# Attention values of all sixteen heads computed ahead of the heads, token-major, and the output units in another order

## The chip, the core and the metric

One NeuronCore of a Trainium2 chip runs the whole kernel as one launch. The metric is the device time of that launch in microseconds (us). Engines are called by their short names in the profile: PE (TensorE, matrix products), DVE (VectorE), ACT (ScalarE), POOL (GpSimd) and SP (SyncE, which here only issues DMAs).

## What is computed

One block over 512 tokens of width 2048, float32. First an RMS norm and a mixer of 16 heads of width 128, then an RMS norm and a sparse expert layer (PEER). The change touches the mixer alone:

```python
proj = rmsnorm(x) @ w_in              # q, k, v, gate of 8 heads; q, k, v of 8 heads; 8 forget logits
# heads 0..7 ("fox"): softmax(q k^T * s + c_q - c_k, causal) @ v, times sigmoid(gate);
#                     q and k are RMS-normed per head
# heads 8..15 ("stick breaking"): a = exp(log_sigmoid(z) + suffix sum of log_sigmoid(-z)) @ v
mixed = concat([fox * sigmoid(gate), sb])
h = x + mixed @ w_out
y = h + peer(rmsnorm(h))
```

## The kernel before

Every large product is made of **units**. A unit is one weight tile of 128 x 2048 float32 (1 MB). SP loads it to `raw[k % 2]` (`load`), ACT rounds it to `wh[k % 2]` (`split_hi`, line 399), and POOL, in the later stages DVE, writes the remainder to `wl[k % 2]` (`split_lo`, line 405). PE then makes 48 matmuls of 512 columns: high by high, high by low and low by high. There are two buffers of each kind, so unit k is loaded after the remainder of unit k-2 is made and rounded after unit k-2 is multiplied. The activations stand in SBUF in the same two parts, `xh` and `xl`.

Two forms of unit exist. `gemm` (lines 419 to 421) has the weights stationary and gives 128 output features by 512 tokens in one PSUM bank. `chunk_unit` (lines 444 to 446) has the activations stationary and gives 128 tokens by 512 output features in each of four banks; four such units (q = 0 to 3) add up to one chunk c of 512 features. The output projection uses `chunk_unit`, 16 units, chunks 0 to 3 one after another.

The mixer runs as follows. After the norm comes a small unit for the forget logits. A fox head has four `gemm` units (q, k, v, gate), a stick-breaking head three (q, k, v), 56 in all. PE's instructions are in an order written out by hand: between the units of head h it does the attention steps of head h-1. For a fox head: `logits_pe`, unit, `vturn_pe`, unit, `pturn_pe`, unit, `out_pe`, `sumsq_pe`, unit. For a stick-breaking head: `z_pe`, unit, `vturn_pe`, `tri_pe`, unit, `out_pe`, unit. `vturn_pe` (line 1800) turns the head's values from feature-major to token-major with four transposes; ACT has copied them out of the bank before (`value_act`, line 886) and DVE copies them again after (`vtok_dve`, line 1174).

Each of ACT and DVE has one queue, worked in order. For a stick-breaking head ACT does the absolute value, exponential and logarithm of the scores (lines 925 to 930) and three rounded copies (933), DVE the softplus (1254, 1259) and three remainders (1262), and PE's `tri_pe` waits for all of them.

After the last `gemm` the output of the heads, `mixed`, which occupies the memory of `acc`, is split again into `xh` and `xl` in four quarters: ACT's `mix_split(k)` (line 971) and DVE's `mix_rest(k)` (line 1294), each over 128 x 2048. Quarter q is read by output units q of every chunk. `xh` can only be overwritten when the last `gemm` is done.

The output units need free banks: ahead of the first matmul into a bank, PE waits on the counter `chunk_out` (the argument `prev` of `chunk_unit`). For chunks 0 and 1 the banks are free from the start, and the counter gets its 8 by one DVE instruction:

```python
nc.vector.memset(stat[:, 12:13], 0.0).then_inc(chunk_out, 8)     # line 1302
```

It stands in DVE's queue behind `mix_rest(0)` and `mixed_dve(NSB - 1)` (the copy of the last head's output), and ahead of `mix_rest(1)`, `(2)` and `(3)`. Once quarter tb of `mixed` is split, SP reloads `x` into `acc[:, tb]`; after the four of them it loads the norm's gain, then the further weights.

Of the kernel before, what the change touches and what calls it, by code (L numbers as in the profile page):

```python
# [87 lines left out]
N_FOX = 1  # L88
N_SB = N_FOX + 4 * NFOX
N_OUT = N_SB + 3 * NSB  # L90
# [10 lines left out]
M_PQ = N_OUT  # L101
# [38 lines left out]
def build(nc, x, attn_g, w_f, w_in, b_forget, q_g, k_g, w_out, ffn_g, ffn_row, w_pq, sub_keys, u, v, u_rows,  # L140
          v_rows, out):
    ctx = ExitStack()
    with ctx:
# [48 lines left out]
        q_raw, k_raw, q_sq, k_sq, qn, kn, vT, gT, vtok = (at(512 * i, 512) for i in range(9))  # L192
# [67 lines left out]
        CHUNK_BANKS = [[banks[6], banks[7], banks[4], banks[5]], banks[0:4]]  # L260
        GATE_BANKS = [banks[6], banks[7], banks[3], banks[1]]
# [48 lines left out]
        vt_done = sem("vt_done")  # L310
        vtok_done = sem("vtok_done")
# [229 lines left out]

        def zero(n):
            return isinstance(n, int) and n <= 0
# [35 lines left out]
        def _(sp):  # L579
# [14 lines left out]

            load(sp, N_OUT, w_out[0])
            load(sp, N_OUT + 1, w_out[1])
            load(sp, N_OUT + 2, w_out[2])
            load(sp, N_OUT + 3, w_out[3])
            for tb in range(TB):
# [3 lines left out]
            with sp.Fori(0, 6) as i:  # L603
                for k in (4, 5):
                    load(sp, N_OUT + k, w_out[i * 2 + k], i, 2)
# [218 lines left out]
        def _(act):  # L824
# [38 lines left out]
            def gate_act(p):  # L863

                act.wait_ge(unit_done, p * 4 + 5)
                wait_from(act, mixed_done, p)
                nc.scalar.activation(gT, gemm_bank[0][:], ACT.Exp, scale=-1.0).then_inc(freed[0], 1)
# [9 lines left out]
            def square_act(h, c):  # L877

                act.wait_ge(freed[(1 + c) % 2], h * 2 + (1 + c) // 2 + 1)
# [3 lines left out]
            def value_act(k, i=0, stride=0):  # L883

                act.wait_ge(unit_done, k + 1 + stride * i)
                nc.scalar.activation(vT, gemm_bank[k % 2][:], ACT.Copy).then_inc(freed[k % 2], 1)
# [7 lines left out]
            def fox_act(h, p):  # L894

                if p is not None:
                    gate_act(p)
                split_hi(act, 2, h, 4)
                if p is not None:
                    exp_act(p)  # L900
                else:
                    forget_act()
# [8 lines left out]
            fox_act(0, None)  # L911
            fox_act(1, 0)
            with act.Fori(2, NFOX) as h:
                fox_act(h, h - 1)
# [27 lines left out]
            def stick_pair_act(i, peeled):  # L942
                for r in range(2):
                    k = N_SB + 3 * r
                    s = i * 2 + r
                    if peeled and r == 0:
                        gate_act(NFOX - 1)
                        split_hi(act, k + 1)
                        exp_act(NFOX - 1)
                        query_act(k)  # L950
                        split_hi(act, k + 2)
                        split_hi(act, k + 3)
                    else:
                        value_act(k - 1, i, 6)
                        split_hi(act, k + 1, i, 6)
                        softplus_act(s - 1)
                        query_act(k, i)
                        split_hi(act, k + 2, i, 6)
                        weight_act(s - 1)
                        split_hi(act, k + 3, i, 6)  # L960

            stick_pair_act(0, True)
            with act.Fori(1, NSB // 2) as i:
                stick_pair_act(i, False)
            softplus_act(NSB - 1)
            value_act(N_OUT - 1)
# [8 lines left out]
            weight_act(NSB - 1)  # L975
            for k in (1, 2, 3):
                mix_split(k)
# [10 lines left out]
            for n in range(N_PQ - N_OUT):  # L988
                split_hi(act, N_OUT + n + 1)
                if n in (5, 9, 13):  # L990
                    for tb in range(TB):
                        chunk_square(n // 4 - 1, tb)
# [130 lines left out]
        def _(dve):  # L1123
# [48 lines left out]
            def vtok_dve(a):  # L1172
                dve.wait_ge(vt_done, a + 1)
                nc.vector.tensor_copy(vtok, banks[7][:]).then_inc(vtok_done, 1)

# [5 lines left out]
            def gate_dve(p):  # L1181

                dve.wait_ge(freed[0], p * 2 + 3)
# [24 lines left out]

            def fox_dve(h, p):
                if p is not None:  # L1210
                    max_dve(p)
                    prob_dve(p)
                else:
                    dve.wait_ge(unit_done, 1)
                    nc.vector.tensor_copy(ftmp, gemm_bank[0][32:32 + PH, :]).then_inc(forget_step, 1)
                    dve.wait_ge(forget_step, 3)
                    nc.vector.tensor_tensor(ftmp, gemm_bank[0][0:PH, :], ftmp, ALU.add).then_inc(forget_step, 1)
                    dve.wait_ge(forget_step, 4)
                    nc.vector.tensor_scalar(flog, ftmp, bf[:, 0:1], None, ALU.add).then_inc(freed[0], 1)
                copy_out(1, q_raw, h, 4)  # L1220
                if p is not None:
                    decay_dve(h)
                    vtok_dve(p)
                copy_out(2, k_raw, h, 4)
                if p is not None:
                    turned_dve(p)
                    gate_dve(p)
                else:

                    dve.wait_ge(decay_ready, 6)  # L1230
                    dve.wait_ge(act_step, 3)
                    nc.vector.scalar_tensor_tensor(out=flog, in0=flog, scalar=0.0, in1=ftmp, op0=ALU.min,
                                                   op1=ALU.subtract).then_inc(dve_step, 1)
                    dve.wait_ge(dve_step, 1)
                    nc.vector.tensor_tensor_scan(csum, cr[0:PH].bitcast(F32), flog, 0.0, ALU.mult,
                                                 ALU.add).then_inc(csum_done, 1)
                    dve.wait_ge(csum_done, 1)
                    nc.vector.tensor_copy(csum_hi, csum).then_inc(csum_done, 1)
                    dve.wait_ge(csum_done, 2)
                    nc.vector.tensor_tensor(csum, csum, csum_hi.bitcast(F32), ALU.subtract).then_inc(csum_done, 1)  # L1240
                    dve.wait_ge(csum_done, 3)
                    decay_dve(h)
                rms_dve(h)

            fox_dve(0, None)
            fox_dve(1, 0)
            with dve.Fori(2, NFOX) as h:
                fox_dve(h, h - 1)
# [16 lines left out]
            def mixed_dve(s):  # L1265
                dve.wait_ge(o_done, s + (NFOX + 1))
                nc.vector.tensor_copy(mixed_at(s + NFOX), banks[6][:]).then_inc(mixed_done, 1)

            def stick_pair_dve(i, peeled):
                for r in range(2):  # L1270
                    k = N_SB + 3 * r
                    s = i * 2 + r
                    if peeled and r == 0:
                        max_dve(NFOX - 1)
                        prob_dve(NFOX - 1)
                        vtok_dve(NFOX - 1)
                        turned_dve(NFOX - 1)
                        copy_out(k + 1, kn)
                        gate_dve(NFOX - 1)
                    else:  # L1280
                        softplus_dve(s - 1)
                        vtok_dve(s + (NFOX - 1))
                        copy_out(k + 1, kn, i, 6)
                        mixed_dve(s - 1)

            stick_pair_dve(0, True)
            with dve.Fori(1, NSB // 2) as i:
                stick_pair_dve(i, False)
            softplus_dve(NSB - 1)
            vtok_dve(HEADS - 1)  # L1290
# [18 lines left out]
            for c in range(CH - 1):  # L1309
                add_chunk(dve, N_OUT + 4 * c + 3, 3 * c, c, CHUNK_BANKS[c % 2])  # L1310
# [460 lines left out]
        def _(pe):  # L1771
# [3 lines left out]
            def sumsq_pe(h):  # L1775

                for c, buf in enumerate((q_sq, k_sq)):
# [17 lines left out]
            def vturn_pe(a, k, i=0, stride=0):  # L1795

                evacuated(pe, k, i, stride)
                wait_from(pe, vtok_done, a)
                for j in range(TB):
# [287 lines left out]
```

## Time and profile before

| | |
|---|---|
| time, median of 3 runs | 3244.74 us (3244.32 to 3246.33) |
| the profiled execution's own time | 3248.89 us |
| its span, first to last instruction | 3247.1 us |
| PE busy | 3217.4 us, 99% |
| mean granted TensorE clock | 0.998 |
| mixer units, first matmul to last | 32.96 to 954.21 us of the span |

A matmul's busy time overlaps the next one's: the records show 0.39 us each, while their starts are 0.23 us apart. What PE's work costs is therefore read from the distance between starts in the timeline, not from the busy time. "Idle before" names whose signal ended a wait.

### The profile page before, as it was taken

What the parts mean: (1) busy time and instruction counts of PE and PEld (TensorE: products, weight loads), DVE (VectorE), ACT (ScalarE), POOL (GpSimd) and SP (SyncE); (2) the same over time, 40 slices, a digit from 0 to 9 for tenths busy, and PEclk for the clock granted to TensorE, in tenths of its full rate; (3) what the DMA queues carried; (4) which work ended last, traced back from release to release, by engine and by line L of the source; (5) the groups of instructions that cost most, each with busy time, mean ns of one, the idle gap of its engine ahead of it and who ended that gap; (6) DMA issues with size and microseconds to landing.
All of it is one profiled execution on the core that took longest, in us unless ns stands there. A gap on an engine that the chain in (4) does not pass through costs nothing. (4 is left out here: it accounts for less than half of the span.)

```text
span 3247.1 us, 41510 instructions
## 1 busy us (share of the span) xinstructions
PE 3217.4 (99%) x16730; PEld 2817.9 (87%) x16730; DVE 2263.5 (70%) x2636; ACT 1123.7 (35%) x1172; POOL 933.5 (29%) x424
## 2 busy tenths in 40 slices
PE   8999999999999999999999999999999999999999
PEld 6878778887878899999999899889989988888887
DVE  5666541113027888988874898888888888888887
ACT  5232323334232234566553223222222322222221
POOL 4333333333433331111101223233323321223222
PEclk9999999999999999999999999999999999999999
DMA  3222222223233247899977999889988988888888
GB/s 144 78 78 90 78 78 79 78 78 136 97 117 118 91 145 270 292 329 321 324 237 266 343 342 348 338 336 351 353 330 326 364 346 308 318 337 340 343 320 317
DMA packets 171364, 777.87 MB, mean 240 GB/s; under 512 B 14064, under 2 KB 80752, under 8 KB 86384
## 3 DMA queue, kind: packets, MB, share of 16 engines
q1 hardware_dynamic: 127488, 457.77, 38.6%
q0 software_dynamic: 43776, 318.79, 26.2%
q8 instruction: 60, 0.98, 0.1%
q14 instruction: 40, 0.33, 0.0%
HBM read 731.10 MB, written 44.34 MB: 239 GB/s over the span
## 5 line engine op out<-in xcount | busy, mean ns | idle before, releaser
L419 PE MATMUL bank<-xh,wh 128*128 128x336 f32 (+1 forms) x3184 | 1105.5, 347 | 1.8 <-DVE wl L1128 1.8
L421 PE MATMUL bank<-xh,wl 128*128 128x336 f32 (+1 forms) x3184 | 1090.1, 342 | 0.0
L420 PE MATMUL bank<-xl,wh 128*128 128x336 f32 (+1 forms) x3184 | 1088.1, 342 | 0.0
L399 ACT ACTIVATE wh<-raw 128x2048 fp32r<-128x2048 f32 x344 | 658.1, 1913 | 1001.9 <-PE bank L446 734.9
L1128 DVE TENSOR_TENSOR wl<-raw,wh 128x2048 fp32r<-128x2048 f32 x252 | 576.8, 2289 | 211.2 <-ACT wh L399 210.0
L419 PEld LDWEIGHTS bank<-xh,wh 128*128 128x128 f32 x3184 | 598.9, 188 | 46.9 <-issue 4.0
L405 POOL TENSOR_TENSOR wl<-raw,wh 128x2048 fp32r<-128x2048 f32 x92 | 425.0, 4620 | 741.3 <-ACT wh L399 741.3
L420 PEld LDWEIGHTS bank<-xl,wh 128*128 128x128 f32 x3184 | 599.2, 188 | 44.8 <-issue 1.9
L421 PEld LDWEIGHTS bank<-xh,wl 128*128 128x128 f32 x3184 | 598.2, 188 | 45.1
L444 PE MATMUL bank<-wh,xh 128*128 128x512 f32 x1072 | 417.1, 389 | 0.8 <-DVE stat L1302 0.8
L446 PE MATMUL bank<-wh,xl 128*128 128x512 f32 x1072 | 417.0, 389 | 0.0
L445 PE MATMUL bank<-wl,xh 128*128 128x512 f32 x1072 | 417.0, 389 | 0.0
L811 POOL DMA_INDIRECT arena<-in_u_rows,g_idx x128 | 251.3, 1963 | 453.5 <-DVE acc L1617 221.8
L811 POOL DMA_INDIRECT arena<-in_v_rows,g_idx x128 | 176.9, 1382 | 610.4 <-DVE acc L1617 314.3
L1596 DVE CUSTOM_DVE_ANT_0 arena<-arena 128x2048 f32<-128x2048 f32 x128 | 291.9, 2288 | 54.6 <-DMA arena<-in_u_rows,g_idx 54.5
L1617 DVE SCALAR_TENSOR_TENSOR acc<-arena,acc 128x2048 f32<-128x2048 f32 x128 | 300.5, 2347 | 3.6 <-DMA arena<-in_v_rows,g_idx 0.3
L444 PE MATMUL bank<-wh,gh 128*128 128x512 f32 x720 | 280.9, 390 | 1.3 <-DVE wl L1128 1.2
L446 PE MATMUL bank<-wh,gl 128*128 128x512 f32 x720 | 280.3, 389 | 0.0
L445 PE MATMUL bank<-wl,gh 128*128 128x512 f32 x720 | 280.2, 389 | 0.0
L444 PEld LDWEIGHTS bank<-wh,xh 128*128 128x128 f32 x1072 | 201.2, 188 | 42.6 <-DVE stat L1302 1.0
L446 PEld LDWEIGHTS bank<-wh,xl 128*128 128x128 f32 x1072 | 201.2, 188 | 41.8
L445 PEld LDWEIGHTS bank<-wl,xh 128*128 128x128 f32 x1072 | 201.2, 188 | 41.8
(211 smaller groups left out, 2804.8 us busy)
## 6 DMA issues: line engine op xcount, KB each, us to landing
raw<-in_u SPq DMA_DIRECT2D x128, 1024.0 KB
raw<-in_v SPq DMA_DIRECT2D x128, 1024.0 KB
raw<-in_w_in SPq DMA_DIRECT2D x56, 1024.0 KB
gate_scratch<-arena SPq DMA_DIRECT2D x12, 2048.0 KB
arena<-gate_scratch SPq DMA_DIRECT2D x32, 768.0 KB, 9.0
raw<-in_w_out SPq DMA_DIRECT2D x16, 1024.0 KB
raw<-in_w_pq SPq DMA_DIRECT2D x16, 1024.0 KB
act_scratch<-arena SPq DMA_DIRECT2D x68, 168.0 KB
```

The costliest lines, as they stand in the source:

```text
L399: nc.scalar.activation(wh[s][:], raw[s][:], ACT.Copy).then_inc(hi_done, 1)
L405: nc.gpsimd.tensor_tensor(wl[s][:], raw[s][:], wh[s][:].bitcast(F32), ALU.subtract).then_inc(lo_done, 1)
L419: nc.tensor.matmul(dst, w_h[:, c], xh[:, c, 0:width], start=(c == 0), stop=False)
L420: nc.tensor.matmul(dst, w_h[:, c], xl[:, c, 0:width], start=False, stop=False)
L421: last = nc.tensor.matmul(dst, w_l[:, c], xh[:, c, 0:width], start=False, stop=(c == KC - 1))
L444: nc.tensor.matmul(bank[:], a_hi(e)[:, rows_], w_h[:, e], start=begin, stop=False)
L445: nc.tensor.matmul(bank[:], a_hi(e)[:, rows_], w_l[:, e], start=False, stop=False)
L446: mm = nc.tensor.matmul(bank[:], a_lo(e)[:, rows_], w_h[:, e], start=False, stop=end)
L811: nc.gpsimd.indirect_dma_start(out=rows_g[n % ROW_BUFS], out_offset=None, in_=table, in_offset=bass.IndirectOffsetOnAxis(ap=g_idx[:, slot: ...
L1128: nc.vector.tensor_tensor(wl[k % 2][:], raw[k % 2][:], wh[k % 2][:].bitcast(F32), ALU.subtract).then_inc(lo_done, 1)
L1596: nc.vector.tensor_tensor_reduce(out=rows_g[b], in0=rows_g[b], in1=x_tok, scale=1.0, scalar=0.0, op0=ALU.mult, op1=ALU.add, accum_out=dots ...
L1617: nc.vector.scalar_tensor_tensor(out=acc[:, DB, :], in0=rows_g[b], scalar=dots[:, GM + j:GM + j + 1], in1=acc[:, DB, :], op0=ALU.mult, op1 ...
```

## The change

The value weights are taken out of the heads and put ahead of them as 16 units of their own, worked in the way of `chunk_unit`, so that the values come out token-major at once. DVE copies them into `mixed`, where each head's values stay until that head's output replaces them. `vturn_pe`, `value_act` and `vtok_dve` fall away. A fox head has three units (q, k, gate), a stick-breaking head two (q, k); there are still 56. The loops over heads are written out. At the end the last head's steps `tri_pe` and `out_pe` stand between output units, `z_pe` ahead of them, and the output units run in another order. The splits of `mixed`, the `memset` and the reloads of `x` are placed anew.

```diff
+M_SHIFT = N_VEND - N_V
+OUT_ORDER = [(0, 0), (0, 1), (0, 2), (1, 0), (0, 3)] + [(1, _q) for _q in (1, 2, 3)] + \
+    [(_c, _q) for _c in (2, 3) for _q in range(4)]
+OUT_LAST = [N_OUT + OUT_ORDER.index((_c, 3)) for _c in range(CH)]
...
+        V_BANKS = [banks[0:4], banks[4:8], banks[0:4], [banks[6], banks[7], banks[0], banks[1]]]
...
# SP
+            for n in range(3):
+                load(sp, N_OUT + n, w_out[n])
+            for tb in range(DB):
+                load_x(tb)
+            for n in (3, 4):
+                load(sp, N_OUT + n, w_out[n])
+            load_x(DB)
             sp.dma_start(x_tok, ffn_row.partition_broadcast(P)).then_inc(gain_loaded, 16)
+            load(sp, N_OUT + 5, w_out[5])
...
# ACT, a fox head
-                split_hi(act, 2, h, 4)
+                split_hi(act, k + 1)
                 if p is not None:
                     exp_act(p)
-                split_hi(act, 3, h, 4)
+                split_hi(act, k + 2)
                 square_act(h, 0)
-                split_hi(act, 4, h, 4)
+                act.wait_ge(unit_done, k + 2)
                 square_act(h, 1)
-                value_act(3, h, 4)
-                split_hi(act, 5, h, 4)
+                split_hi(act, k + 3)
                 rms_act(h)
...
# ACT, the end
             mix_split(0)
-            weight_act(NSB - 1)
-            for k in (1, 2, 3):
+            split_hi(act, N_OUT + 1)
+            softplus_act(NSB - 1)
+            for k in (1, 2):
                 mix_split(k)
...
-            for n in range(N_PQ - N_OUT):
+            for n in range(1, N_PQ - N_OUT):
                 split_hi(act, N_OUT + n + 1)
+                if n == 2:
+                    weight_act(NSB - 1)
+                if n == 3:
+                    mix_split(3)
...
# DVE, values
+            def value_dve(c):
+
+                dve.wait_ge(unit_done, N_V + 4 * c + 4)
+                heads = mixed[:, c * D:(c + 1) * D].rearrange("p (h t n) -> p h t n", h=4, t=TB)
+                for tb in range(TB):
+                    nc.vector.tensor_copy(heads[:, :, tb, :], V_BANKS[c][tb][:].rearrange("p (h n) -> p h n", h=4)
+                                          ).then_inc(v_out, 1)
...
# DVE, the end
             mix_rest(0)
+            softplus_dve(NSB - 1)
+            for k in (1, 2):
+                mix_rest(k)
+            nc.vector.memset(stat[:, 12:13], 0.0).then_inc(chunk_out, 8)
             mixed_dve(NSB - 1)
-
-            nc.vector.memset(stat[:, 12:13], 0.0).then_inc(chunk_out, 8)
-            for k in (1, 2, 3):
-                mix_rest(k)
+            mix_rest(3)
...
# PE
+            for c in range(CH):
+                for q in range(4):
+                    chunk_unit(pe, N_V + 4 * c + q, V_BANKS[c], q == 0, q == 3, lambda e: xh[:, 4 * q + e, :],
+                               lambda e: xl[:, 4 * q + e, :], lambda tb: v_free(c, tb))
...
+            for s in range(NSB):
+                stick_pe(s)
+            z_pe(NSB - 1)
+
+            def chunk_free(c, tb):
+
+                pe.wait_ge(chunk_out, 4 * c + tb + 1)
+                if c == 1 and tb == DB:
+                    pe.wait_ge(mixed_done, HEADS)
+
+            for n, (c, q) in enumerate(OUT_ORDER):
+                if n == 2:
+                    tri_pe(NSB - 1)
+                if n == 3:
+                    out_pe(HEADS - 1, at_done, 4 * NSB)
+                pe.wait_ge(mix_lo, q + 1)
+                chunk_unit(pe, N_OUT + n, CHUNK_BANKS[c % 2], q == 0, q == 3, lambda e: xh[:, 4 * q + e, :],
+                           lambda e: xl[:, 4 * q + e, :], lambda tb: chunk_free(c, tb), each=True, by_block=q == 3)
```

## Rows read from the trace of the kernel before

**Rows 1.** The page: busy time of PE, and the group of POOL's remainders.
```profile
PE 3217.4 (99%) x16730; PEld 2817.9 (87%) x16730; DVE 2263.5 (70%) x2636; ACT 1123.7 (35%) x1172; POOL 933.5 (29%) x424
...
L405 POOL TENSOR_TENSOR wl<-raw,wh 128x2048 fp32r<-128x2048 f32 x92 | 425.0, 4620 | 741.3 <-ACT wh L399 741.3
```
**Rows 2.** Timeline (start, duration, instruction, idle before) of PE and DVE, fox heads.
```profile
170.34 1.88 PE L1781 MATMUL bank<-arena,ones 128*128 128x512 f32 x4
...
172.81 6.57 DVE L1203 RECIPROCAL arena<-arena 128x512 f32<-128x512 f32 x2 [1.39 <-ACT arena L891]
...
182.96 0.39 PE L1790 MATMUL bank<-arena 128*128 128x128 f32 x2
...
197.15 0.60 PE L1800 MATMUL bank<-ident,arena 128*128 128x128 f32 x4
...
208.53 1.25 PE L1807 MATMUL bank<-ident,arena 128*128 128x128 f32 x10
```
**Rows 3.** Timeline of PE, one stick-breaking head.
```profile
700.90 0.60 PE L1800 MATMUL bank<-ident,arena 128*128 128x128 f32 x4
701.25 0.48 PE L1864 MATMUL bank<-gh,gl 128*128 128x512 f32 x1
...
704.47 0.47 PE L419 MATMUL bank<-xh,wh 128*128 128x512 f32 x1
...
715.48 2.32 PE L1817 MATMUL bank<-arena 128*128 128x512 f32 x8
717.56 0.48 PE L419 MATMUL bank<-xh,wh 128*128 128x512 f32 x1
...
728.53 1.02 PE L1851 MATMUL bank<-arena 128*128 128x512 f32 x2
```
**Rows 4.** Timeline of PE, from the last `gemm` to the first output unit.
```profile
760.40 0.48 PE L419 MATMUL bank<-xh,wh 128*128 128x512 f32 x1
...
772.22 0.66 PE L1800 MATMUL bank<-ident,arena 128*128 128x128 f32 x4 [0.69 <-ACT arena L886]
...
779.99 0.50 PE L444 MATMUL bank<-wh,xh 128*128 128x512 f32 x1 [0.81 <-DVE stat L1302]
```
**Rows 5.** Timeline of PE, the first instruction after the 16 output units.
```profile
954.21 0.27 PE L496 MATMUL bank<-ident,arena 128*128 128x128 f32 x1
```
**Rows 6.** Timeline of ACT: a square, the softplus of a head, a split of `mixed`.
```profile
210.55 0.61 ACT L881 ACTIVATE arena<-arena 128x512 f32<-128x512 f32 x1
...
731.03 1.41 ACT L925 ACTIVATE arena<-bank 128x512 f32<-128x512 f32 x4
...
738.31 1.08 ACT L933 ACTIVATE gh<-arena 128x384 fp32r<-128x384 f32 x2 [0.16 <-DVE arena L1259]
...
772.07 1.90 ACT L971 ACTIVATE xh<-acc 128x2048 fp32r<-128x2048 f32 x1
```
**Rows 7.** Timeline of DVE: last remainders of a softplus, a head's output, the end.
```profile
739.38 1.49 DVE L1262 TENSOR_TENSOR gl<-arena,gh 128x512 fp32r<-128x512 f32 x3
...
758.64 0.69 DVE L1267 COPY acc<-bank 128x512 f32 x1 [1.58 <-PE bank L1817]
...
774.00 2.29 DVE L1294 TENSOR_TENSOR xl<-acc,xh 128x2048 fp32r<-128x2048 f32 x1 [0.40 <-ACT xh L971]
...
779.86 0.06 DVE L1302 MEMSET stat<- 128x1 f32 x1
```
**Rows 8.** Busy time by stretch, PE's granted clock third from the end.
```profile
1757.70:1759.50 1.80, 0.00 (x0) 0.00 (x0) 1.80 (x2) 1.80 (x3) 0.00 (x0) 1.00 0.01 5
...
1760.74:1764.16 3.42, 3.42 (x14) 3.42 (x14) 3.42 (x3) 0.00 (x0) 0.00 (x0) 0.50 0.70 283
```
**Rows 9.** DMA issues from 765 to 840 us: count, size, median us to landing.
```profile
acc<-in_x SPq DMA_DIRECT2D x4, 1024.0 KB, 10.0
arena<-in_ffn_row SPq DMA_DIRECT2D x1, 1024.0 KB, 14.7
```
**Rows 10.** All of line 1294: duration in ns, shortest, median and longest.
```profile
L1294 DVE TENSOR_TENSOR xl<-acc,xh x4: 2285/2289/6692, 774.0 to 784.2; 128x2048 fp32r<-128x2048 f32 x4
```

More of the change, by code:

```diff
@@ L940, in weight_act, with stick_act @@
                                          ACT.Exp).then_inc(at_done, 1)
[L942 to L966, printed above, removed]
+            def stick_act(s):
+                k = N_SB + 2 * s
+                if s == 0:
+                    gate_act(NFOX - 1)
+                    split_hi(act, k + 1)
+                    exp_act(NFOX - 1)
+                    query_act(k)
+                    split_hi(act, k + 2)
+                else:
+                    split_hi(act, k + 1)
+                    softplus_act(s - 1)
+                    query_act(k)
+                    split_hi(act, k + 2)
+                    weight_act(s - 1)
+            for s in range(NSB):
+                stick_act(s)
             act.wait_ge(unit_done, N_OUT)
@@ L1212, in fox_dve @@
                     prob_dve(p)
[L1213 to L1220, printed above, removed]
+                copy_out(k, q_raw)
                 if p is not None:
                     decay_dve(h)
-                    vtok_dve(p)
-                copy_out(2, k_raw, h, 4)
+                    turned_dve(p)
+                copy_out(k + 1, k_raw)
                 if p is not None:
-                    turned_dve(p)
                     gate_dve(p)
[L1228 to L1242, printed above, removed]
-                rms_dve(h)
[L1245 to L1248, printed above, removed]
+                rms_dve(h)
+            forget_dve()
+            for c in range(CH):
+                value_dve(c)
+            for h in range(NFOX):
+                fox_dve(h, h - 1 if h else None)
             def softplus_dve(s):
@@ L1266, in mixed_dve, with stick_dve @@
                 dve.wait_ge(o_done, s + (NFOX + 1))
[L1267 to L1290, printed above, removed]
+                nc.vector.tensor_copy(mixed_at(s + NFOX), out_bank(s + NFOX)[:]).then_inc(mixed_done, 1)
+            def stick_dve(s):
+                k = N_SB + 2 * s
+                if s == 0:
+                    max_dve(NFOX - 1)
+                    prob_dve(NFOX - 1)
+                    turned_dve(NFOX - 1)
+                    copy_out(k + 1, kn)
+                    gate_dve(NFOX - 1)
+                else:
+                    softplus_dve(s - 1)
+                    copy_out(k + 1, kn)
+                    mixed_dve(s - 1)
+            for s in range(NSB):
+                stick_dve(s)
             def mix_rest(k):
@@ L1834, in fox_pe, with z_pe @@
                 sumsq_pe(h)
-                gemm(pe, 4, 4, h, 4, 4)
-            fox_pe(0, None)
-            fox_pe(1, 0)
-            with pe.Fori(2, NFOX) as h:
-                fox_pe(h, h - 1)
-            def z_pe(s, k, i=0):
-                evacuated(pe, k, i, 6)
-                evacuated(pe, k + 1, i, 6)
-                if isinstance(s, int) and s == 0:
+                gemm(pe, k + 2, m + 2)
+            for h in range(NFOX):
+                fox_pe(h, h - 1 if h else None)
+            def z_pe(s):
+                m = N_SB + 2 * s - M_SHIFT
+                evacuated(pe, m)
+                evacuated(pe, m + 1)
+                if s == 0:
                     pe.wait_ge(pt_out, 4 * NFOX)
@@ L1874, in tri_pe @@
                                      skip_group_check=True).then_inc(tri_done, 1)
-            def stick_pair_pe(i, peeled):
-                for r in range(2):
-                    k = N_SB + 3 * r
-                    s = i * 2 + r
-                    if peeled and r == 0:
-                        logits_pe(NFOX - 1)
-                        gemm(pe, k, k)
-                        vturn_pe(NFOX - 1, 3, NFOX - 1, 4)
-                        pturn_pe(NFOX - 1)
-                        gemm(pe, k + 1, k + 1)
-                        out_pe(NFOX - 1, pt_out, 4 * NFOX)
-                        gemm(pe, k + 2, k + 2)
-                    else:
-                        z_pe(s - 1, k - 3, i)
-                        gemm(pe, k, k, i, 6, 6)
-                        vturn_pe(s + (NFOX - 1), k - 1, i, 6)
-                        tri_pe(s - 1)
-                        gemm(pe, k + 1, k + 1, i, 6, 6)
-                        out_pe(s + (NFOX - 1), at_done, s * 4)
-                        if isinstance(s, int) and s == NSB - 1:
-                            z_pe(s, k, i)
-                        gemm(pe, k + 2, k + 2, i, 6, 6)
@@ L1899, in _, with stick_pe @@
-            stick_pair_pe(0, True)
-            with pe.Fori(1, NSB // 2 - 1) as i:
-                stick_pair_pe(i, False)
-            stick_pair_pe(NSB // 2 - 1, False)
-            vturn_pe(HEADS - 1, N_OUT - 1)
-            tri_pe(NSB - 1)
-            out_pe(HEADS - 1, at_done, 4 * NSB)
-            with pe.Fori(0, 2) as w:
-                for r in range(2):
-                    for q in range(4):
-                        pe.wait_ge(mix_lo, q + 1)
-                        chunk_unit(pe, N_OUT + 4 * r + q, CHUNK_BANKS[r], q == 0, q == 3,
-                                   lambda e: xh[:, 4 * q + e, :], lambda e: xl[:, 4 * q + e, :],
-                                   lambda tb: pe.wait_ge(chunk_out, w * 8 + 4 * r + tb + 1), w, 8, each=True,
-                                   by_block=q == 3)
+            def stick_pe(s):
+                k = N_SB + 2 * s
+                m = k - M_SHIFT
+                if s == 0:
+                    logits_pe(NFOX - 1)
+                    gemm(pe, k, m)
+                    pturn_pe(NFOX - 1)
+                    gemm(pe, k + 1, m + 1)
+                    out_pe(NFOX - 1, pt_out, 4 * NFOX)
+                else:
+                    z_pe(s - 1)
+                    gemm(pe, k, m)
+                    tri_pe(s - 1)
+                    gemm(pe, k + 1, m + 1)
+                    out_pe(s - 1 + NFOX, at_done, s * 4)
```

124 lines of the change are left out of this document (73 added, 51 removed).

## The prediction, made blind

> **What bounds the kernel now.** I read the page's engine lines first: PE is busy 99% of the span [rows 1]. So the time is PE's work plus PE's waits, and the other engines count only where PE waits for them. Since matmuls overlap, I then went by starts in PE's timeline. A unit of the output projection costs (954.21 - 779.99) / 16 = 10.89 us [rows 4, 5], that is 48 steps of 0.227 us. Between units stand the attention steps, and inside the mixer they run without a wait: a fox head and a stick-breaking head repeat to 0.01 us. PE's only waits in this stretch lie at its end: 0.69 us for ACT's copy of the last values and 0.81 us for the `memset` of line 1302 [rows 4], and one of the same size between them. That last releaser matters most here: PE already waits for the counter that DVE's queue gives, and the change moves that instruction.
>
> **What is removed.** A fox head loses one `gemm` and one `vturn_pe`: from line 1800 to line 1807 it is 208.53 - 197.15 = 11.38 us [rows 2], seven times 79.7. The first head has no attention steps yet and loses a bare unit, 10.9. A stick-breaking head loses the transposes, 701.25 - 700.90 = 0.35, and the unit after `out_pe`, 728.53 - 717.56 = 10.97 [rows 3], together 11.32, for seven heads (s = 0 to 6) 79.2, with 0.1 more in the first. The last stick-breaking head loses its transposes, 0.35, and at the end everything between 760.40 and 779.99 that isn't `tri_pe` or `out_pe`: 19.59 [rows 4] less 704.47 - 701.25 = 3.2 and 717.56 - 715.48 = 2.1 [rows 3] leaves 14.3, in which are its value unit, the last transposes and the three waits, about 2.1 us of waits. Sum 79.7 + 10.9 + 79.3 + 14.6 = 184.5 us.
>
> **What is added in work.** 16 units by `chunk_unit`: 16 x 10.89 = 174.2 us [rows 4, 5]. `tri_pe` and `out_pe` now each break a run of output units; the unit after such a step costs 10.97 and not 10.89 [rows 3, 5], twice 0.1. So PE's own work and old waits fall by 184.5 - 174.2 - 0.2 = 10.1 us. DVE's 16 copies of values (0.7 us each by [rows 7]) lie beside units. Only the fourth chunk comes back to a bank (its third block) that was just used: PE gets there 6 x 0.227 = 1.4 us after the third chunk, the copy is made after about 0.9. Nothing, at most 0.5 us.
>
> **New wait 1: the first head's squares.** `copy_out(k + 1)` and the square of k now come right after that unit, ahead of `sumsq_pe`. Copy 0.69 [rows 7] and square 0.61 [rows 6] with some 0.25 us of signals make 1.55 us; the first half of `sumsq_pe` covers 0.65. In later heads `out_pe` (2.1 us) covers it. Cost 0.9 us, once.
>
> **Chains that stay covered.** The norm of q and k: the reciprocals of line 1203 take 6.57 us, and from `sumsq_pe` to the next logits there are 182.96 - 170.34 = 12.62 us [rows 2]. In the new order DVE first does the gate's reciprocal, 3.3 us, after `copy_out(k + 1)`, and ends at about 5 us from the unit's end; ACT's roots are there at 5.4, the two reciprocals end at 11.9, the products at 13.3, and PE arrives after 2.2 + 12.6 = 14.8. 1.5 us to spare; in the first head, which has no `out_pe`, 0.3. The softplus: in the last cycle but one it ran from 731.03 to 739.38 + 1.49 = 740.87 [rows 6, 7]; in the new order it ends some 1.9 us before `tri_pe` needs it, 1.2 us in the old one. I put nothing on either; at worst 0.5 to 1 us for each of seven heads.
>
> **New wait 2, the large one: the gate of the output units.** Count from E, when PE leaves the last `gemm`. PE does `out_pe`, 2.1 us, and `z_pe`, 2.1 us, and stands before output unit 0 at E + 4.2. That unit needs `chunk_out`, which comes only from the `memset`. In DVE's queue this now stands behind `softplus_dve` of the last head and behind `mix_rest(1)` and `mix_rest(2)`. Their chain:
> ACT starts at E + 0.2 with `mix_split(0)`, 1.9 [rows 6], then the rounding of a weight, again 1.9, less 0.1 of overlap each, and begins the last softplus at E + 3.8. From that first absolute value to the last rounded copy ACT needs 738.31 + 1.08 - 731.03 = 8.36 us [rows 6]: E + 12.1. Then `mix_split(1)` to E + 14.0, `mix_rest(1)` of 2.29 [rows 7] to E + 16.2, `mix_rest(2)` to E + 18.5, then the `memset`, and PE starts 0.1 later, as in [rows 4, 7]. PE waits 18.6 - 4.2 = 14.4 us. Nothing else hides it: PE's queue has only output units next, and all are behind the same wait. The mixed quarter that unit 0 itself needs is ready at E + 5.4.
>
> **The clock after it.** The granted clock is a cost of its own. After 1.8 us without a matmul, up to 1759.5 us, it was 0.50 of full, the lower of the two levels (1.2 GHz), from 1760.74 to 1764.16 us [rows 8]. So it came back 4.7 us after PE had resumed. After 14 us of idleness I expect it low from the first matmul and for as long, 4.7 us at half speed: 2.4 us lost. Bounds: 1.7 (the 3.4 us of that row) and 3.4 (twice that).
>
> **New wait 3: output unit 5.** Its weights are now loaded behind the last reload of `x` and behind the gain. `mix_rest(3)` must come first. Counted from the end of output unit 2: `out_pe` 2.5 to its signal, the copy 0.7, `mix_split(3)` 1.9: 5.1. POOL meanwhile makes the remainder of unit 4's weights until about 6.8 (4.6 us [rows 1]). `mix_rest` beside such a POOL instruction took 6.69 us and not 2.29 [rows 10], so I take that it starts only at 6.8 and ends at 9.1. Then three transfers of 1 MB: the gain, sixth of a burst, landed 14.7 us after its issue and the four `x` at 10.0 in the middle [rows 9], some 2.45 us for each one more, so the third of a burst lands about 9.8 us after the first issue: 18.9. Rounding 1.9 and POOL 4.6 make 25.5. PE is there after 2.1 + 11.0 + 10.9 = 24.0. Wait 1.4 us; between 0 and 3, as the landing is an estimate from [rows 9]; a second fall of the clock would add about 1.7.
>
> The Trainium skill, page "SBUF — State Buffer", section "Who interferes with whom", says that a VectorE instruction with two SBUF inputs and a GpSimd one that reads SBUF exclude each other for the whole of whichever started first. The 6.69 us of [rows 10] agree with it. Without that rule `mix_rest(3)` would end at 7.4, wait 3 would be nil, and the sum 1.4 us lower.
>
> **The sum.** -10.1 (work and old waits) + 0.9 + 14.4 + 2.4 + 1.4 = +9.0 us. Against the profiled execution that is 3248.89 + 9.0 = 3257.9 us. The median of the runs is 4.15 us below that execution, so the forecast for it is 3244.74 + 9.0 = 3253.7, or 0.28% slower. What a measurement of this kernel can tell from no change is about 0.2%, 6.5 us: "same" is 3238.3 to 3251.2.
>
> **The rivals.**
> 1. *The gate does not hold PE* (faster). If unit 0 is held only by its own quarter of `mixed`, at E + 5.4, wait 2 is 1.2 us and there is hardly a clock cost: -10.1 + 0.9 + 1.2 + 1.4 = -6.6, so 3238. It decides once DVE reaches the `memset` before E + 5.5. Against it: the 0.81 us of [rows 4] are a wait for this very instruction, and DVE works its queue in order. Chance 0.07.
> 2. *The gate holds, but its chain is shorter or the rest of the costs are not paid* (within 0.2%). If the clock costs 1.7, wait 3 nothing and wait 2 13.5, the sum is +6.0: 3250.7. Below about 6.5 us of net cost the result is "same". Chance 0.17.
> 3. *The chains with little to spare are late as well.* With two or three units per head, the norm or the softplus comes 0.5 us late in most heads, 15 x 0.5 = +7 us more at worst, or the clock falls a second time at wait 3, +1.7: 3255.5 to 3261. For it: margins of 0.3 to 1.9 us. Against it: the old margins were of like size and held every time. Chance 0.13.
> 4. *The forecast:* one wait of 14 us with its clock, small ones beside it, 3251.2 to 3257. Chance 0.63.
>
> So faster 0.07, same 0.17, slower 0.76. Range: 3248.5 (the lower bounds of all three waits and a little more) to 3260 (rival 3 for the most part); what is left out is rival 1 and the far end of rival 3.
>
> **What would show it.** In the changed kernel's PE timeline: 16 units of 10.89 us at the start; heads of about 41.0 and 29.4 us between logits or `z_pe`; after the last `z_pe` an idle of some 14 us ended by DVE's `memset`, the granted clock at half for 3 to 7 us after it; some 1.4 us of idle ahead of the sixth output unit, ended by POOL. Wrong would be: no idle there, the `memset` early in DVE's timeline, or waits of PE inside the heads.

## The result

The changed kernel takes 3254.59 us (median of 7 runs, 3252.9 to 3259.53), the kernel before in the same session 3244.32 (7 runs). The ratio is 1.0036, with a 95% interval of 1.0027 to 1.0045: 0.36% slower, 10.3 us by the medians. Forecast were 3253.7 us and 9.0 us. Of all runs in this document one, of the kernel of "The weights of output unit 5 ahead of the burst", took 9617.44 us, for a reason that nothing here shows, and is left out as a slow run.

The changed kernel's lines are shifted: `gemm` is 425 to 427, `chunk_unit` 450 to 452, `mix_split` 975, `mix_rest` 1302, the `memset` 1311, POOL's remainder 411. The page first, as [rows 1]:

```profile
span 3251.2 us, 40906 instructions
PE 3207.6 (99%) x16666; PEld 2810.4 (86%) x16666; DVE 2227.2 (69%) x2636; ACT 1117.6 (34%) x1156; POOL 932.8 (29%) x424
```

PE is busy 9.8 us less and the kernel is slower, and the page's engine line can't show why. All of PE's waits inside the mixer and the output units are these, from the list of who waited for whom:

```profile
PE bank L450 <- DVE stat L1311: 14.2, 1, 14.2
PE bank L450 <- POOL wl L411: 3.0, 1, 3.0
...
PE bank L1792 <- ACT arena L897: 0.6, 1, 0.6
```

Columns: engine, what it was about to do, whom it waited for, total us, how often, the longest. Three waits, the three that were forecast. PE's timeline has them in place (start, duration, instruction, idle before):

```profile
32.25 0.39 PE L450 MATMUL bank<-wh,xh 128*128 128x512 f32 x1
...
206.34 0.39 PE L425 MATMUL bank<-xh,wh 128*128 128x512 f32 x1
...
229.77 1.13 PE L1792 MATMUL bank<-arena,ones 128*128 128x512 f32 x2 [0.65 <-ACT arena L897]
...
719.83 0.47 PE L425 MATMUL bank<-xh,wh 128*128 128x512 f32 x1
...
749.18 0.47 PE L425 MATMUL bank<-xh,wh 128*128 128x512 f32 x1
...
760.19 2.32 PE L1820 MATMUL bank<-arena,acc 128*128 128x512 f32 x8
762.35 2.32 PE L1865 MATMUL bank<-arena 128*128 128x512 f32 x8
778.83 0.76 PE L450 MATMUL bank<-wh,xh 128*128 128x512 f32 x1 [14.16 <-DVE stat L1311]
...
843.86 0.47 PE L450 MATMUL bank<-wh,xh 128*128 128x512 f32 x1 [3.01 <-POOL wl L411]
...
965.25 0.27 PE L502 MATMUL bank<-ident,arena 128*128 128x128 f32 x1
```

The value units take 206.34 - 32.25 = 174.1 us. A stick-breaking head repeats after 749.18 - 719.83 = 29.35 us. The mixer with the output projection lasts 965.25 - 32.25 = 933.0 us; before it was 954.21 - 32.96 = 921.25 [rows 5]. So it grew by 11.75 us. In the profiled executions the span grew by only 4.1. The rest of the kernel was 7.0 us longer in the old one, where the clock fell to half twice, for 6.8 us from 958.6 and for 3.4 us from 1760.7 ([rows 8] is the second); at half speed these 10.2 us lose 5.1. The medians of the runs are the better witness of the total, and the length of the mixer in the trace of the cause.

"Gate" is the name from here on for the `memset` that lets the output units begin. DVE's queue at the end of the mixer, beside [rows 7]:

```profile
763.15 2.28 DVE L1302 TENSOR_TENSOR xl<-acc,xh 128x2048 fp32r<-128x2048 f32 x1
769.41 0.69 DVE L1268 SCALAR_TENSOR_TENSOR arena<-bank,arena 128x512 f32<-128x512 f32 x1 [3.98 <-ACT arena L941]
...
772.33 1.49 DVE L1276 TENSOR_TENSOR gl<-arena,gh 128x512 fp32r<-128x512 f32 x3
774.17 4.49 DVE L1302 TENSOR_TENSOR xl<-acc,xh 128x2048 fp32r<-128x2048 f32 x2 [0.35 <-ACT xh L975]
778.61 0.06 DVE L1311 MEMSET stat<- 128x1 f32 x1
```

`mix_rest(0)`, then four idle microseconds while ACT works on the softplus, the softplus, two more quarters of `mixed`, and only then the instruction that PE waits for: 778.61 - 760.19 = 18.4 us after the last `gemm`, where 18.5 were forecast. The quarter that the first output unit needs was ready at 765.4.

The clock, busy time by stretch (PE first, its granted clock third from the end), as [rows 8]:

```profile
764.70:778.80 14.10, 0.00 (x0) 0.00 (x0) 9.50 (x15) 9.79 (x11) 5.10 (x1) 0.67 0.29 95
769.40:778.80 9.40, 0.00 (x0) 0.00 (x0) 8.77 (x14) 5.17 (x5) 0.40 (x1) 0.50 0.14 37
778.80:783.03 4.23, 4.20 (x10) 3.36 (x11) 0.00 (x0) 0.00 (x0) 0.00 (x0) 0.50 1.00 413
783.03:800.00 16.97, 16.97 (x76) 14.05 (x76) 0.00 (x0) 1.92 (x1) 4.59 (x1) 1.00 0.19 70
...
844.50:847.90 3.40, 3.40 (x10) 2.63 (x9) 0.00 (x0) 0.00 (x0) 3.40 (x1) 0.50 0.84 296
```

The clock fell to half 4.7 us into the idleness and stayed there for 4.2 us of PE's work, and it fell once more after the third wait.

### The profile page after: what moved, and what is told of

Its sections match the earlier page's. It is cut to its first block, busy times and chain, and to the rows that moved or that the text cites. A ratio compares the mean times of both kernels' runs of the same rounds, so it can differ in the third digit from the quotient of the medians.

```text
span 3251.2 us, 40906 instructions
## 1 busy us (share of the span) xinstructions
PE 3207.6 (99%) x16666; PEld 2810.4 (86%) x16666; DVE 2227.2 (69%) x2636; ACT 1117.6 (34%) x1156; POOL 932.8 (29%) x424
## 4 chain that ended last, share of the span: by engine, by line
PE 65%; issue 22%; POOL 5%; DMA 4%; DVE 3%; ACT 2%; POOLq 0%; SPq 0%; ACTq 0%; DVEq 0%
PE bank L450 12%; PE bank L452 12%; PE bank L451 12%; PE bank L427 9%; PE bank L425 9%; PE bank L426 9%; POOL wl L411 4%; DMA raw<-in_u 2%; PE bank L1978 2%; DMA arena<-in_u_rows,g_idx 1%; DVE wl L1137 1%; ACT wh L405 1%; DMA acc<-in_u_rows,arena 1%; DVE acc L1503 1%; PE bank L1933 0%
## 5 line engine op out<-in xcount | busy, mean ns | idle before, releaser
L425 PE MATMUL bank<-xh,wh 128*128 128x336 f32 (+1 forms) x2928 | 1003.8, 343 | 0.3 <-DVE wl L1137 0.3
L427 PE MATMUL bank<-xh,wl 128*128 128x336 f32 (+1 forms) x2928 | 989.7, 338 | 0.0
L426 PE MATMUL bank<-xl,wh 128*128 128x336 f32 (+1 forms) x2928 | 987.8, 337 | 0.0
L425 PEld LDWEIGHTS bank<-xh,wh 128*128 128x128 f32 x2928 | 550.3, 188 | 35.8 <-issue 2.5
L450 PE MATMUL bank<-wh,xh 128*128 128x512 f32 x1328 | 518.7, 391 | 18.4 <-DVE stat L1311 14.2
L452 PE MATMUL bank<-wh,xl 128*128 128x512 f32 x1328 | 518.0, 390 | 0.0
L451 PE MATMUL bank<-wl,xh 128*128 128x512 f32 x1328 | 517.9, 390 | 0.0
L450 PEld LDWEIGHTS bank<-wh,xh 128*128 128x128 f32 x1328 | 250.2, 188 | 71.4 <-DVE xl L1302 14.3
L452 PEld LDWEIGHTS bank<-wh,xl 128*128 128x128 f32 x1328 | 250.1, 188 | 52.2
L451 PEld LDWEIGHTS bank<-wl,xh 128*128 128x128 f32 x1328 | 250.3, 188 | 51.8
```

The lines of the kernel that those rows point to most:

```text
L425: nc.tensor.matmul(dst, w_h[:, c], xh[:, c, 0:width], start=(c == 0), stop=False)
L426: nc.tensor.matmul(dst, w_h[:, c], xl[:, c, 0:width], start=False, stop=False)
L427: last = nc.tensor.matmul(dst, w_l[:, c], xh[:, c, 0:width], start=False, stop=(c == KC - 1))
L450: nc.tensor.matmul(bank[:], a_hi(e)[:, rows_], w_h[:, e], start=begin, stop=False)
L451: nc.tensor.matmul(bank[:], a_hi(e)[:, rows_], w_l[:, e], start=False, stop=False)
L452: mm = nc.tensor.matmul(bank[:], a_lo(e)[:, rows_], w_h[:, e], start=False, stop=end)
```

## The experiments

The theory under test: the values ahead of the heads save some 10 us; the place of one `memset` in DVE's queue takes 14 of them back and the clock two more; a burst of DMAs takes the rest. Against it stand: the first output unit is held by the splitting or the softplus themselves, whatever the `memset` does; or shorter heads hide less. "Mixer" is its length in the trace, as above; times are medians. The eight kernels were run in two groups of four, each with the kernel before beside it, and the ratios are to that. It took 3244.16 us beside the gate ahead of everything, the gate half way, the weights of unit 5 ahead of the burst and both mends, and 3243.73 beside the other four. The changed kernel was not run again in either group; the kernel before was 0.2 and 0.6 us faster there than beside it, so of each difference to the changed kernel below that much is not the edit's. Where a second figure stands "against each one's own kernel before", this is taken off.

### The gate ahead of everything

```diff
+            nc.vector.memset(stat[:, 12:13], 0.0).then_inc(chunk_out, 8)
             mix_rest(0)
             softplus_dve(NSB - 1)
             for k in (1, 2):
                 mix_rest(k)
-            nc.vector.memset(stat[:, 12:13], 0.0).then_inc(chunk_out, 8)
```

> The changed kernel with one edit: DVE's memset that lets the output units begin stands ahead of mix_rest(0). Theory (the gate): PE's wait before output unit 0 falls from 14.2 us to the 1.1 us until mix_rest(0) has ended, the granted clock stays full there, so 13.1 + 2 = 15 us less than the changed kernel: about 3239.5, ratio to the kernel before 0.9985. Rival (the split): if unit 0 was held by the splitting of mixed or by the softplus itself, the wait stays near 14 us and the time near 3254.6. Rival (the heads): if the loss came from heads with fewer units to hide behind, nothing moves either.

Measured: 3238.82 us (11 runs), ratio to the kernel before 0.9985 (0.9976 to 0.9994). Mixer 917.45 us, 15.55 less than in the changed kernel. PE's first output unit:

```profile
766.03 0.50 PE L450 MATMUL bank<-wh,xh 128*128 128x512 f32 x1 [0.84 <-DVE xl L1302]
```

Now it waits for the split that it needs, 0.84 us. Moving one instruction of 0.06 us gains 15.8 us by the medians (15.6 against each one's own kernel before) and turns the sign of the change. Both rivals fall: neither the splitting nor the softplus held the unit, and the heads are untouched by this edit.

### The gate half way

```diff
             mix_rest(0)
             softplus_dve(NSB - 1)
+            nc.vector.memset(stat[:, 12:13], 0.0).then_inc(chunk_out, 8)
             for k in (1, 2):
                 mix_rest(k)
-            nc.vector.memset(stat[:, 12:13], 0.0).then_inc(chunk_out, 8)
```

> The changed kernel with the memset between softplus_dve of the last head and mix_rest(1). Theory (the gate): in the changed kernel's trace the softplus ends 4.8 us ahead of the memset, so PE's wait falls from 14.2 to about 9.5 us and the time by about 4.8, to 3249.8; the clock's loss stays, as 9.5 us of idleness are still enough for it to fall. If the clock's fall needed the longer wait, 2 us more are gained. Rival (the split or the heads): nothing moves.

Measured: 3248.12 us (11 runs), ratio 1.0013 (1.0005 to 1.0022). The wait is as long as the queue ahead of the `memset`:

```profile
774.16 0.77 PE L450 MATMUL bank<-wh,xh 128*128 128x512 f32 x1 [9.32 <-DVE stat L1309]
...
839.74 0.47 PE L450 MATMUL bank<-wh,xh 128*128 128x512 f32 x1 [2.69 <-POOL wl L411]
```

The mixer is 5.9 us shorter than in the changed kernel: 4.85 of them are the wait. The first two output units took 24.7 us instead of 23.8, so the clock's price is not less after a shorter wait. The remaining 1.9 are 0.3 of a shorter wait at output unit 5 and 1.6 of the clock, which didn't fall after that wait this time. That is luck.

```profile
836.90:839.70 2.80, 0.15 (x1) 0.00 (x0) 0.69 (x1) 1.91 (x1) 2.80 (x2) 1.00 0.00 0
839.70:846.00 6.30, 6.26 (x28) 5.21 (x29) 0.00 (x0) 0.00 (x0) 4.45 (x1) 1.00 0.59 190
```

### The gate alone, in the old kernel

```diff
             mixed_dve(NSB - 1)
-            nc.vector.memset(stat[:, 12:13], 0.0).then_inc(chunk_out, 8)
             for k in (1, 2, 3):
                 mix_rest(k)
+            nc.vector.memset(stat[:, 12:13], 0.0).then_inc(chunk_out, 8)
```

> The kernel before with one edit: its memset stands behind mix_rest(3) instead of ahead of mix_rest(1). Theory (the gate alone, without values ahead or a new order): in the old trace mix_rest(3) ended at 790.9 us, so the first output unit starts near 791.0 instead of 779.99, 11 us later, and the clock falls and costs about 2: 3244.2 + 13 = 3257. Rival: with the old order PE finds other work or the clock stays full, and less than 11 us are lost.

Measured: 3255.73 us (5 runs), ratio 1.0038 (1.0024 to 1.0052), 12 us slower. Nothing else of the change is in this kernel. A late gate alone is enough for a loss of this size.

```profile
791.29 0.79 PE L444 MATMUL bank<-wh,xh 128*128 128x512 f32 x1 [11.71 <-DVE stat L1304]
```

The mixer is 934.3 us, 13.0 more than before: 10.9 of wait (11.71 instead of the 0.81 of [rows 4]) and about 2.1 in the 16 output units, 176.38 instead of 174.22 us, at a clock that had fallen.

### Work in place of the wait

```diff
             z_pe(NSB - 1)
+            for _ in range(60):
+                nc.tensor.matmul(banks[7][:], xh[:, 12, 0:P], xh[:, 13, :], start=True, stop=True)
```

> The changed kernel with 60 matmuls of 512 columns, whose results are thrown away, in PE's queue between the last z_pe and output unit 0, that is inside the 14.2 us wait. Theory (the clock is a cost of its own): they take 60 x 0.227 = 13.6 us, less than the wait, so the first output unit still starts at the same time, but the granted clock stays full and the first two output units take 21.8 us and not 23.8: 2 us less than the changed kernel, 3252.6. The wait at output unit 5 stays. Rival: the two units were slow for another cause, then they stay at 23.8 us.

Measured: 3250.82 us (10 runs), ratio 1.0022 (1.0013 to 1.0032), 3.8 us less than the changed kernel by the medians (3.2 against each one's own kernel before); the mixer, 930.0 us, is 3.0 shorter. Busy time by stretch:

```profile
764.70:778.80 14.10, 14.02 (x63) 11.29 (x61) 9.62 (x14) 10.22 (x12) 5.62 (x1) 1.00 0.26 85
778.80:800.00 21.20, 20.74 (x92) 17.22 (x93) 0.30 (x2) 1.92 (x1) 4.59 (x1) 1.00 0.42 171
```

PE still waits 0.5 us for the same `memset`, so the first output unit starts at the same step as before, but at full clock, and the first two units take 21.84 instead of 23.80 us. So 2.0 us of the loss are the clock's, shown by themselves. About 1 us more, which I had not forecast, comes from the wait at output unit 5, 2.1 instead of 3.0 us: SP issued the same four transfers at the same distances, and the weights landed 10.4 us after the first of them and not 11.4 (the cause is read under "DVE and POOL kept apart").

```profile
824.25 0.33 SPq L607 DMA_DIRECT2D acc<-in_x  x1
...
834.66 1.92 ACT L405 ACTIVATE wh<-raw 128x2048 fp32r<-128x2048 f32 x1 [14.45 <-DMA raw<-in_w_out]
```

### The weights of output unit 5 ahead of the burst

```diff
+            load(sp, N_OUT + 5, w_out[5])
             load_x(DB)
             sp.dma_start(x_tok, ffn_row.partition_broadcast(P)).then_inc(gain_loaded, 16)
-            load(sp, N_OUT + 5, w_out[5])
```

> The changed kernel with one edit in SP's queue: the weights of output unit 5 are loaded ahead of the last reload of x and of the gain. Theory: the 3.0 us that PE waits there for POOL vanish, and with them the second fall of the clock (3.4 us at half, 1.7 lost): 4.7 us less, 3249.9. Rival: the wait is POOL's own, from sharing with mix_rest(3), and stays; or the last reload of x comes too late for the first chunk's addition and a wait arises one unit later, and the time stays within 1 us of 3254.6.

Measured: 3251.73 us (8 runs, 3248.34 to 3254.66), ratio 1.0025 (1.0014 to 1.0035). In the trace the wait is gone, units 3 to 15 take 141.56 instead of 146.44 us, and the mixer is 928.6 us, 4.4 shorter. In the runs 2.9 of these are seen (2.7 against each one's own kernel before). The profiled execution, 3254.01 us, is one of the slowest of the eight: its clock fell twice later on (965.7 and 1573.2 us), and the first two output units took 24.3 instead of 23.8 us after the same wait of 14.16. The two next kernels, whose mixers are as long and whose traces have the first of these falls too (at 964.5 and 964.7 us), got the whole gain. The intervals of the three ratios overlap, so whether this kernel really gains less is not shown.

### The gain behind the weights

```diff
             load_x(DB)
-            sp.dma_start(x_tok, ffn_row.partition_broadcast(P)).then_inc(gain_loaded, 16)
             load(sp, N_OUT + 5, w_out[5])
+            sp.dma_start(x_tok, ffn_row.partition_broadcast(P)).then_inc(gain_loaded, 16)
```

> The changed kernel with one edit in SP's queue: the weights of output unit 5 behind the last reload of x still, but ahead of the gain. Theory (the burst of transfers sets wait 3): in the changed kernel's trace the weights landed 4.1 us after the gain, so they land about 4 us earlier and the 3.0 us wait is gone; the time is that of the kernel with the load ahead of both, near 3252. Rival (mix_rest(3) sets it alone): only the 2.5 us of one transfer are gained and 0.5 us of the wait stay.

Measured: 3249.43 us (10 runs), ratio 1.0018 (1.0008 to 1.0027), 5.2 us less than the changed kernel (4.6 against each one's own kernel before) and 2.6 less than expected; no wait at output unit 5, mixer 928.3 us, 4.7 shorter. ACT's rounding starts when the weights land, in the changed kernel and in this one:

```profile
837.18 1.92 ACT L405 ACTIVATE wh<-raw 128x2048 fp32r<-128x2048 f32 x1 [15.44 <-DMA raw<-in_w_out]
```

```profile
833.51 1.92 ACT L405 ACTIVATE wh<-raw 128x2048 fp32r<-128x2048 f32 x1 [11.37 <-DMA raw<-in_w_out]
```

The burst began at 825.79 and 826.18 us. As second of the burst the weights are there after 7.3 us, as third after 11.4: one transfer less ahead gains 4.1 us and not 2.5, and the wait is gone altogether. The rival's half microsecond doesn't show; 1.6 of the 4.1 us are the late last part of the third transfer in the changed kernel, of which more in the next experiment.

### DVE and POOL kept apart

```diff
+                if n == 3:
+                    mix_split(3)
                 split_hi(act, N_OUT + n + 1)
                 if n == 2:
                     weight_act(NSB - 1)
-                if n == 3:
-                    mix_split(3)
```

> The changed kernel with one edit in ACT's queue: mix_split(3) stands ahead of the rounding of output unit 4's weights, so that POOL's remainder starts only after mix_rest(3) has begun. Theory (DVE and POOL shut each other out): mix_rest(3) takes 2.3 us instead of 4.0, the reload of x is issued 1.7 us earlier, and the wait at output unit 5 falls from 3.0 to 1.3 us. Rival (no exclusion): mix_rest(3) stays at 4.0 us and the wait at 3.0.

Measured: 3249.66 us (10 runs), ratio 1.0019 (1.0009 to 1.0028), 4.9 us less than the changed kernel (4.3 against each one's own kernel before); mixer 928.6 us, 4.4 shorter. First all of line 1302 in the changed kernel (shortest, median, longest), then `mix_rest(3)` here:

```profile
L1302 DVE TENSOR_TENSOR xl<-acc,xh x4: 2281/2289/3984, 763.2 to 821.8; 128x2048 fp32r<-128x2048 f32 x4
```

```profile
L1302 DVE TENSOR_TENSOR xl<-acc,xh x1: 2293/2293/2293, 822.3 to 822.3; 128x2048 fp32r<-128x2048 f32 x1
```

3.98 us became 2.29, as expected. But the wait fell to nothing and not to 1.3 us. SP's issues and the landings say why, changed kernel first:

```profile
825.79 0.33 SPq L607 DMA_DIRECT2D acc<-in_x  x1
826.16 0.43 SPq L616 DMA_DIRECT2D arena<-in_ffn_row  x1
826.63 1.12 SPq L397 DMA_DIRECT2D raw<-in_w_out  x2
```

```profile
824.61 0.33 SPq L607 DMA_DIRECT2D acc<-in_x  x1
824.98 0.43 SPq L616 DMA_DIRECT2D arena<-in_ffn_row  x1
825.46 4.11 SPq L397 DMA_DIRECT2D raw<-in_w_out  x2
...
834.46 1.92 ACT L405 ACTIVATE wh<-raw 128x2048 fp32r<-128x2048 f32 x1 [10.40 <-DMA raw<-in_w_out]
```

The third transfer, unit 5's weights, landed 837.18 - 825.79 = 11.4 us after the burst began in the changed kernel and 834.46 - 824.61 = 9.85 us here. So 1.7 of the 3.0 us are gained by the earlier issue (counted from the start of output unit 3), and 1.5 by the quicker landing. The fourth transfer doesn't explain this, though here it is issued 3.8 us behind the third and there at once: in the kernel with both mends nothing is issued behind the third, and by its records it landed 11.3 us after the first issue.

The DMA records show what does differ. The semaphore of a transfer counts 16 parts. The first part of the third transfer landed 9.1 to 9.5 us after the first issue in all eight traces of the changed kernel and its variants, and only the last one or two parts came late. In the changed kernel a fetch of instructions, 16 KB, fell into the burst 8.8 us after the first issue. Here it began 11.1 us after it, when the third transfer had landed. The DMA queues from the first issue to that landing (packets, MB, share of the 16 engines), changed kernel first; the fetch of 16 KB is q8, and q14 is another of 8 KB:

```profile
q1 hardware_dynamic: 551, 4.10, 89.1%
q8 instruction: 1, 0.02, 0.6%
q14 instruction: 1, 0.01, 0.2%
```

```profile
q1 hardware_dynamic: 481, 3.55, 89.2%
q14 instruction: 1, 0.01, 0.2%
```

In the other traces it is the same. Where the fetch of 16 KB began 8.6 to 8.9 us after the first issue (changed kernel, gate ahead, gate half way, weights ahead, both mends), the third transfer landed after 11.0 to 11.4 us. Where it began after 9.7 us (gain behind the weights), the third transfer, here the gain, landed after 10.3 and the fourth had the part that came 1.4 us late. In the filler's trace it had come before the burst, and the only late part, 0.8 us, followed the fetch of 8 KB. The old kernel's burst, from which [rows 9] come, met no fetch (its row from 788 to 808.6 us is the only one), and no part of it was more than 0.2 us behind the middle one:

```profile
q1 hardware_dynamic: 1008, 7.34, 86.6%
```

No run moved a fetch and nothing else, so the cause is read from ten traces that agree, and not isolated by an experiment.

### Both mends together

The edits of the first experiment and of "the weights of output unit 5 ahead of the burst".

> Both edits: memset ahead of mix_rest(0), weights of output unit 5 ahead of the last reload of x. Theory: the two gains add up, 15 + 4.7 us less than the changed kernel: about 3235, ratio to the kernel before 0.997, which is the 10 us of removed work and old waits less 0.6 for the first head's squares and 1.1 for mix_rest(0). Rival: with the units 15 us earlier something else comes late (mix_rest(1) ends just as unit 1 begins; a load waits for the third reload of x), and less than 15 us are gained in all: 3239 or more.

Measured: 3233.59 us (5 runs, 3230.99 to 3234.67), ratio to the kernel before 0.9968 (0.9955 to 0.9981): 0.32% faster than it and 21 us faster than the changed kernel. The trace has no fall of the clock between the start and the end of PE's work:

```profile
core 0: 3232.6 us, clock 1.000
```

PE's waits in the mixer are 0.8 us for `mix_rest(0)` and 0.6 for the squares. The mixer takes 913.07 us, 8.2 less than before. That is the worth of the change once nothing takes it back, the two old waits for the last values and the old gate included, and this kernel beats both. The parts of the change were not run apart.

## Why the prediction was right, step by step

The sum was for the mixer, so it is set against the mixer's 11.75 us.

- **Removed and added work:** forecast -10.1. What is left of the 11.75 when the other terms are taken off is 11.75 - 14.4 - 2.0 - 4.9 - 0.9 = -10.45. The kernel with both mends gives it without the large terms: its mixer is 8.2 us shorter than before, with 0.9 for the squares and 1.1 for `mix_rest(0)` in it, which leaves -10.2. The heads came to 29.35 us (29.4 forecast) and the value units to 174.1 (174.2).
- **The first head's squares:** forecast 0.9. The step through `sumsq_pe` grew from 1.31 to 2.23 us, 0.9; the profile calls 0.65 of it idle. Right.
- **The gate:** forecast 14.4, measured 14.4 from start to start (14.16 of idleness). The step that carried the argument was reading DVE's queue in order and asking what PE is told by each instruction of it; [rows 4] already showed PE waiting for that `memset`. Three experiments put the instruction elsewhere, and the wait followed it each time.
- **The clock after it:** forecast 2.4, measured 2.0, and 2.0 again by the filler run. It came back 4.2 us after PE resumed, where [rows 8] had given 4.7. In the three other traces with the same wait (the weights of unit 5 ahead, the gain behind them, DVE and POOL apart) it came back after 4.6 to 5.2 us, at a price of 2.1 to 2.4.
- **The wait at output unit 5:** the mechanism was right, the term was too small: forecast 1.4, measured 3.2 from start to start (3.0 idle), and 1.7 more for a second fall of the clock, which I had named and not counted. The mis-sized term is the landing of the weights: 9.8 us after the burst's first issue in the forecast, 11.4 measured. The 9.8 was worked out from [rows 9], a burst that no fetch of instructions met. Of the eight traces with the new burst only the one in which the fetch of 16 KB came behind the third transfer gave it, 9.85.
- **Exclusion of DVE and POOL:** I took it that `mix_rest(3)` starts only when POOL's instruction has ended, and so ends 9.1 us after output unit 2; it ended after 9.0. It took 3.98 us beside POOL and 2.29 us apart from it, in two kernels that differ in the order of two ACT instructions. The Trainium skill, page "SBUF — State Buffer", section "Who interferes with whom", says that the two shut each other out, and these traces agree. By the measured terms the sum without it would be 1.7 us smaller, not 1.4, and a wait of 1.3 us would be left.
- **Chains said to be covered:** no wait for the norm or the softplus in any head, so the first part of rival 3 fell; its second part, a second fall of the clock at wait 3, came true with the 1.7 us that it gave.
- **The total:** +10.3 by the medians, +9.0 forecast. The nearness of the two is in part luck: the sum was for the mixer, which grew by 11.75, wait 3 and its clock being 3.5 us too small and the other terms together 0.75 too large, and the medians show 1.5 us less than the mixer. The rest of the kernel after the mixer, 2285.9 us in the changed kernel's trace and 2292.9 in the old one's, differs by clock falls and small waits that moved between the profiled executions (it was 2284.7 to 2286.7 in seven others and 2290.7 in one); it isn't counted as an effect of the change.

Rival 1, that the gate doesn't hold PE, was wrong for this kernel, and its mechanism came true once the `memset` was moved: 3238.82 measured where the rival's sum gave 3238. That the numbers are so near is luck as well, since wait 3 was 2.8 us there and not the sum's 1.4, with a fall of the clock behind it.

## What to carry to other kernels

When a step is moved down an in-order queue, list every signal that the instructions behind it give, not only the data that they make; an instruction of 0.06 us whose only work is a count can cost 14 us. A saving of PE work is best checked against the first place where PE meets another engine's queue after it, since all of it can be lost there in one wait, and the clock adds its own price. And a load that is moved behind a burst of others should get its margin from several executions, and from bursts with a fetch of instructions in them, not from the mean pace of one.

## What the runs showed of the hardware that I had not expected

- A wait of 2 to 3 us may or may not be followed by a fall of the clock. After 3.0 us of idleness (changed kernel) and 2.8 (gate first) it fell to half for 3.4 us, and even after 2.1 (filler) too; after 2.7 (gate half way) it did not. The same idle pattern at the second norm, 5.86 us for its first 16 transposes, was followed by 6.8 us at half clock in the old kernel's trace and by none in the changed one's (from the first transpose to the next stage, 24.8 and 22.3 us). It was followed by a fall in four of the ten traces.
- A fetch of 16 KB of instructions that fell into a burst of 1 MB loads while other transfers were still to land was followed, in all twelve such cases from 755 to 870 us of the ten traces, by one part in 16 that landed 1.4 to 1.9 us behind the middle ones, and the transfers behind it in the burst had such a part too. Without such a fetch no part there was more than 1.1 us behind. A wait for the whole transfer pays for that one part.
- The price of the clock after a long wait was 2.0 to 2.4 us after 14.2 us of idleness (four traces), 2.2 after 11.7 and 2.9 after 9.3 (one each), so here it didn't grow with the wait.
